# Probability blocks as weights for two column halves of the array, and the first block's logits in one piece

## The reference

```python
def block(i):                      # 128 queries at a time
    ...
    _, sel = lax.top_k(score, top_k)
    ...
    logits = jnp.einsum('bqhd,bqkhd->bhqk', qa, ks).astype(jnp.float32) * scale
    ...
    p = jax.nn.softmax(logits, axis=-1).astype(vs.dtype)
    return jnp.einsum('bhqk,bqkhd->bqhd', p, vs)
```

## Time and profile before

| | |
|---|---|
| time, median of 3 runs | 505.52 us (505.5 to 505.55) |
| time of the profiled execution | 505.5 us |
| its span | 503.8 us |
| granted TensorE clock, mean | 0.996 |
| TensorE matmul busy | 492.6 us (98%) |
| VectorE, ScalarE, GpSimd busy | 372.5, 253.4, 334.5 us |
| products, line 2094 | 160 records, 21.4 us, from 174.3 to 254.8 us |
| logits, line 2071 | 128 records, 13.7 us, from 169.8 to 243.9 us |

### The profile page before, as it was taken

One profiled execution on the slowest core, in us unless ns is written; L12 is line 12 of the kernel. 1 busy time (PEld: TensorE's weight loads), 2 busy tenths in 40 slices (PEclk: granted clock), 3 DMA queues, 4 the chain that ended last, 5 costly groups with the idle time before them and its releaser, 6 DMA issues.

```text
span 503.8 us, 8288 instructions
## 1 busy us (share of the span) xinstructions
PE 492.6 (98%) x3121; PEld 396.8 (79%) x3121; DVE 372.5 (74%) x770; ACT 253.4 (50%) x416; POOL 334.5 (66%) x206
## 2 busy tenths in 40 slices
PE   7999999999999999999999999999999999999994
PEld 7975888778888788888888879887777778788883
DVE  3795499689997447566497274999999999848814
ACT  6733854331332433734476546557776656447303
POOL 5470659769994285656429946869999999940701
PEclk9999999999999999999999999999999999999998
DMA  8357225176458122202370533608777772501004
GB/s 277 106 170 252 85 83 168 23 273 241 157 232 282 53 85 84 85 1 83 119 301 15 154 83 85 167 16 196 190 187 179 180 193 87 203 15 69 0 1 167
DMA packets 50741, 67.36 MB, mean 134 GB/s; under 512 B 4616, under 2 KB 32291, under 8 KB 49678
## 3 DMA queue, kind: packets, MB, share of 16 engines
q1 hardware_dynamic: 50702, 66.84, 42.8%
HBM read 58.76 MB, written 7.91 MB: 132 GB/s over the span
## 4 chain that ended last, share of the span: by engine, by line
PE 91%; POOL 3%; DVE 2%; ACT 2%; issue 1%; POOLq 0%; ACTq 0%
PE bank L1851 36%; PE bank L1871 26%; PE bank L2184 7%; PE bank L2094 3%; PE bank L2071 3%; PE bank L2246 2%; PE bank L2233 2%; PE bank L2083 2%; PE bank L2008 1%; PE bank L1887 1%; PE bank L1786 1%; PE bank L1935 1%; PE bank L2027 1%; POOL w_lo L671 1%; PE bank L1796 1%
## 5 line engine op out<-in xcount | busy, mean ns | idle before, releaser
L671 POOL TENSOR_TENSOR w_lo<-w_raw,w_hi 128x2048 fp32r<-128x2048 f32 (+1 forms) x30 | 136.3, 4546 | 54.8 <-ACT w_hi L873 53.8
L1851 PE MATMUL bank<-hT_hi,w_hi 128*128 128x512 f32 (+1 forms) x280 | 110.5, 395 | 0.0
L1851 PE MATMUL bank<-hT_lo,w_hi 128*128 128x512 f32 (+1 forms) x280 | 110.5, 395 | 0.0
L1851 PE MATMUL bank<-hT_hi,w_lo 128*128 128x512 f32 (+1 forms) x280 | 109.8, 392 | 0.0
L1871 PE MATMUL bank<-w_hi,hT_hi 128*128 128x512 f32 x188 | 76.7, 408 | 0.0
L873 ACT ACTIVATE w_hi<-w_raw 128x2048 fp32r<-128x2048 f32 (+1 forms) x35 | 65.7, 1880 | 15.7 <-PE bank L1871 9.3
L1871 PE MATMUL bank<-w_hi,hT_lo 128*128 128x512 f32 x188 | 73.5, 391 | 0.0
L1871 PE MATMUL bank<-w_lo,hT_hi 128*128 128x512 f32 x188 | 73.4, 390 | 0.0
L1655 DVE SCALAR_TENSOR_TENSOR bank<-r_va,pvec,bank 128x512 f32<-128x512 f32 x94 | 69.1, 754 | 2.2
L1851 PEld LDWEIGHTS bank<-hT_lo,w_hi 128*128 128x128 f32 (+1 forms) x280 | 52.3, 187 | 16.0 <-issue 5.5
L1851 PEld LDWEIGHTS bank<-hT_hi,w_hi 128*128 128x128 f32 (+1 forms) x280 | 52.3, 187 | 12.9 <-issue 1.6
(11 more groups left out here) (284 smaller groups left out, 905.8 us busy)
## 6 DMA issues: line engine op xcount, KB each, us to landing
w_raw<-in_w_in_even_dram SPq DMA_DIRECT2D x14, 1024.0 KB, 5.4
w_raw<-in_w_in_odd_dram SPq DMA_DIRECT2D x16, 512.0 KB, 5.2
r_x<-in_w_out_even_dram SPq DMA_DIRECT2D x5, 1024.0 KB, 7.5
t_kept<-r_x SPq DMA_DIRECT2D x4, 1024.0 KB, 5.3
w_raw<-in_w_in_odd_dram SPq DMA_DIRECT2D x4, 1024.0 KB, 8.1
w_raw<-in_w_out_odd_dram SPq DMA_DIRECT2D x4, 1024.0 KB, 5.1
r_att<-u_kept SPq DMA_DIRECT2D x12, 258.0 KB, 4.5
r_ka<-u_kept SPq DMA_DIRECT2D x12, 258.0 KB, 4.6
```

Source lines behind the costliest of these rows:

```text
L671: nc.gpsimd.tensor_tensor(v(w_lo[j % 3]), v(raw(j)), v(w_hi[j % 3]).bitcast(F32), ALU.subtract).then_inc(lo_ready, 1)
L1851: ins = nc.tensor.matmul(proj_bank(g)[0:m, :], w[:, k, P * i:P * i + m], h[:, k, :], start=(n == 0), stop=(n == 3 * KC - 1))
```

## The change

The product takes each probability block in two halves of 64 queries. Each half is loaded as weights of 128 rows x 64 columns onto one half of the array's columns and writes to one half of the partitions of bank 7. The values are streamed twice, once for each half. In block 0 the logits matmuls take all 128 keys in one piece instead of two of 64.

```diff
@@ qk_pair
-                for c0, c1 in ((0, w // 2), (w // 2, w)):
+                for c0, c1 in ((0, w // 2), (w // 2, w)) if tb else ((0, w),):
                     for i in range(2):
                         ins = nc.tensor.matmul(bank[4 + i][:, c0:c1],
@@ pv
                 for i in range(tb + 1):
-                    ins = nc.tensor.matmul(bank[7][:, AD * h:AD * h + AD], probT[n % 2][:, P * i:P * i + P],
-                                           va[:, i, AD * h:AD * h + AD], start=(i == 0), stop=(i == tb))
+                    for q0 in (0, 64):
+                        ins = nc.tensor.matmul(bank[7][q0:q0 + 64, AD * h:AD * h + AD],
+                                               probT[n % 2][:, P * i + q0:P * i + q0 + 64],
+                                               va[:, i, AD * h:AD * h + AD], start=(i == 0), stop=(i == tb))
                 ins.then_inc(pv_done, 1)
```

## The result

The changed kernel takes 506.91 us (median of 10 runs, 506.23 to 507.22), the kernel before 505.65 us beside it (505.5 to 506.58). The ratio is 1.0019, interval 1.0011 to 1.0028: some 1 us slower. The forecast was 505.2 us, with a range from 504.3 to 506.9; the measured median lies at the very top of it, 0.01 us outside. The profiled execution took 506.39 us, its span is 504.6 us.

A forecast was written before the change was run, and what follows sets the result against it. The prediction took TensorE's own instruction order, paced by weight loads, to bound the attention stage. It summed 505.5 us + 0.41 for the column halves - 0.68 for the unsplit logits to 505.2 us, range 504.3 to 506.9.

The forecast's parts named there:

- What bounds the kernel: In the attention stage TensorE is busy throughout; its instruction order and 128x128 weight loads set the pace, 0.223 us a key block.
- the rule of the crossings: Where TensorE's array division changes, the next start stands 0.07 us short of the last record's duration; entry 0.20, out 0.148.
- Part 1: Products of probabilities times values in two column halves: 0.116 us instead of 0.223 a key block, +0.41 us with division changes.
- Part 2: Block 0's logits unsplit, 8 matmuls of 128 columns instead of 16 of 64: four times -0.17, together -0.68 us.
- Rivals 1 to 5: Alternatives: costlier way out (0.13), no draining (0.06), halves loading in turn (0.04), loads awaiting matmuls (0.02), unsplitting saves nothing (0.05).
- Rival 1: Way out of the column halves costs 0.20 us instead of 0.15, on 30 products: 506.8 us, chance 0.13.
- the Sum: Whole kernel: 505.5 us + 0.41 for the products - 0.68 for the logits = 505.2 us.
- rival 4: Column halves share all rows, a load waits for the other half's matmul: 0.42 us a key block, 530 us, chance 0.02.

The follow-up runs named there:

- the part alone: Against the kernel before: for the product, only its two column halves, 506.35 us; for the logits, only block 0's logits in one piece, 505.03 us.

## Why the prediction was wrong

**What bounds the kernel, and the rule of the crossings: right.** The entry into the column halves costs 0.20 us from the last transpose, the way out 0.15, the second whole-array matmul comes 0.34 behind the first. All three had been read off other divisions of the array and hold for this one.

**Part 1: right.** Two 128x64 loads work side by side at 0.058 us a set. The sum was +0.41 us, the part alone measured +0.43 in its stage. 8.6 us of weight loading are gained and the crossings take them back.

**Part 2: right.** -0.68 forecast, -0.62 measured in the stage, and 505.03 us for the part alone against 504.8.

**Rivals 1 to 5: none of them happened.** Rival 1 gives 506.8 us, nearly the measured number, and is wrong: the way out costs 0.15 us (246.87 to 247.02), not 0.20, and in the attention nothing was lost. A number that fits is no proof of a mechanism; only the trace tells these two apart.

**The step that failed is the Sum,** in which 0.27 us less in the attention was carried unchanged to the end of the span. It holds for 158 us and then fails at one place. I had read the waits of TensorE over the whole run and taken their absence for slack. They show only that nothing waited. In the kernel before, the last read of the rows of chunk 7 landed 0.20 us before the taps, where 0.09 is the least seen. So this chain had 0.11 us of slack, and a delay of 1.5 us in its store, less this slack and the 0.2 us by which the last read was quicker, became 1.2 us of standing. The sum had no term for it: what it put at nothing measured 1.2 to 1.7 us. The forecast also named no transfer as moved by the change, since the kernel's own transfers were not. The stream of TensorE's instructions is one more user of the DMA engines, and the change made it longer by 288 instructions in the trace (8288 to 8576). In the trace of before it was to be seen as one line of the queues on the page (q8, 25 packets of 16 KB); where they fall against the stores was not looked up.

The Trainium skill (page "Runtime: NRT & Kernel Launch", section "Instruction fetch mechanics") says that instructions are refilled in blocks of 16 KiB through a DMA queue of the sequencer's own, and that this cost is mostly hidden. The packets here have that size. They are hidden from TensorE, as it says (in the kernel before, with 25 of them, every listed wait of its matmuls is put down to another engine), but not from the data: each lasted 0.9 to 1.7 us, and the store that met it landed up to 2.1 us late.

That it was the number of instructions that moved the fetch, and not the different times in the attention, is shown by the old kernel with added waits: its stage is unchanged, and its fetch fell from 414.7 to 403.3 us. The exact rule, how many instructions move it how far, stays open. 14 added instructions moved this fetch by 0.9 us and the two ahead of it by 1.5 and 1.7, but the one behind it came 2.7 us later. 53 moved it by 11.4 us in the old kernel, and in the one with column halves only in places the nearest two by 7 and 4.5. The 288 of the change moved it by 11.0, or by that and some whole fetches.

## What to carry to other kernels

Cost a change of how the array is divided at its crossings, not at its matmuls: here a product of one key block between whole-array neighbours lost 0.23 us and each further block gained 0.107, so it pays from four blocks on. Where the division changes behind it anyway, 0.09 us is lost with one block, two are even, and it pays from three on. Before a small gain is carried to the end, look for the chains of transfers that arrive just in time, by the time from the last landing to the first use and not by the list of waits, and put some work in front of their reader. When instructions are added to a long unrolled kernel, its instruction fetches move against its transfers; the same kernel with a few dummy instructions tells such an effect from that of the edit.

## What was unexpected of the hardware

A 16 KB fetch of instructions holds up the packets of a 260 KB store that are still to go, nine of them here, until it has ended, while the rest of the store had gone out in 0.8 us. The store landed after 3.6 and 4.2 us where the fetch ended late in it, 2.4 where it ended at its beginning, 2.1 without.

The weight loads of line 2246 and of the column halves start while matmuls on the same rows run (as far as the records tell, whose ends are modelled), for the column halves one pair behind the other at 0.058 us. The rule that is quoted with rival 4 (the Trainium skill, page "TensorE: Matmul & The Clock Gate", section "The mechanism"), that such overlap needs different row groups, is not what this chip did; the same section also lets a load run ahead into a background weight buffer, and whether that happened here no run shows.
